# SSD gating and norm inside the first inverse, exponents on ScalarE, and the SSD rows of the output product as f16 products

## What is computed

```python
y = _ssd_chunked(xh, dt, A, Bm, Cm) + d_skip[:, None] * xh      # SSD, 8 heads
y = y.reshape(b, T, SSD_D) * jax.nn.silu(z)                      # gate
y = y.reshape(b, T, SSD_GROUPS, SSD_D // SSD_GROUPS)
y = y * lax.rsqrt(jnp.mean(y * y, axis=-1, keepdims=True) + NORM_EPS)   # group norm
y_ssd = y.reshape(b, T, SSD_D) * norm_g
...
y_rwkv = _rwkv7_mixer(...)                     # a delta rule: needs an inverse per chunk
mix = jnp.concatenate([y_ssd, y_rwkv], axis=-1) @ w_out[l]
h = h + _rms_norm(mix, post_mix_norm[l])
...
u = _causal_dwconv(hn @ ffn_w_up[l], ...)
f = (jax.nn.silu(gate) * val) @ ffn_w_down[l]
```

## Time and profile before

| | us |
|---|---|
| runs, median (lowest, highest) | 769.1 (766.74, 769.5) |
| the profiled execution | 765.5 |
| its span, first to last instruction | 763.7 |
| TensorE busy in the span | 741.5 (97%) |
| VectorE busy | 559.7 (73%) |
| ScalarE busy | 423.1 (55%) |
| GpSimd busy | 61.7 (8%) |

### The profile page before, as it was taken

One profiled execution on the slowest core, in us unless ns is written; L12 is line 12 of the kernel. 1 busy time (PEld: TensorE's weight loads), 2 busy tenths in 40 slices (PEclk: granted clock), 3 DMA queues, 4 the chain that ended last, 5 costly groups with the idle time before them and its releaser, 6 DMA issues.

```text
span 763.7 us, 16837 instructions
## 1 busy us (share of the span) xinstructions
PE 741.5 (97%) x7250; PEld 603.2 (79%) x7250; DVE 559.7 (73%) x906; ACT 423.1 (55%) x673; POOL 61.7 (8%) x104
## 2 busy tenths in 40 slices
PE   9999889889999999999999999999999999999997
PEld 7888777779868888888886777788878888865554
DVE  4799977663978999998666986899766576663443
ACT  6699452222664666667555763297554566653442
POOL 0000123030021011101002000002002000000000
PEclk9999989999999999999999999999999999999999
DMA  9990252111393456545791563338336065555101
GB/s 320 397 369 22 90 213 99 40 61 56 118 323 111 154 180 219 220 169 201 244 389 46 191 247 116 111 112 329 113 111 221 1 221 222 221 220 180 70 1 55
DMA packets 67145, 129.47 MB, mean 170 GB/s; under 512 B 3968, under 2 KB 28032, under 8 KB 66816
## 3 DMA queue, kind: packets, MB, share of 16 engines
q1 hardware_dynamic: 66032, 126.07, 45.4%
q0 software_dynamic: 320, 1.64, 0.6%
q10 hardware_dynamic: 720, 0.70, 0.3%
HBM read 127.35 MB, written 1.05 MB: 168 GB/s over the span
## 4 chain that ended last, share of the span: by engine, by line
PE 65%; DVE 20%; ACT 9%; DMA 3%; issue 2%; SPq 0%; DVEq 0%
PE bank L590 19%; PE bank L706 14%; PE bank L2971 11%; DVE arena L541 8%; DVE arena L2274 3%; PE bank L2361 3%; PE bank L1437 3%; DMA ring<-in_w_in_dram 3%; PE bank L809 2%; PE bank L700 2%; ACT arena L532 2%; PE bank L1456 1%; PE bank L2842 1%; PE bank L2823 1%; PE bank L1694 1%
## 5 line engine op out<-in xcount | busy, mean ns | idle before, releaser
L541 DVE SCALAR_TENSOR_TENSOR arena<-ring,arena 128x1024 f16<-128x1024 f32 x194 | 228.3, 1221 | 71.1 <-ACT arena L532 70.8
L590 PE MATMUL bank<-hg,arena 128*128 128x256 f16 x2496 | 276.1, 273 | 0.9 <-DVE arena L541 0.9
L590 PEld LDWEIGHTS bank<-hg,arena 128*128 128x128 f16 x2496 | 243.0, 98 | 33.3 <-issue 3.1
L532 ACT ACTIVATE arena<-ring 128x1024 f16<-128x1024 f32 x194 | 191.9, 1043 | 88.1 <-PE bank L2971 37.6
L2971 PE MATMUL bank<-arena 128*128 128x512 f16 (+1 forms) x480 | 83.6, 336 | 0.0
L2971 PEld LDWEIGHTS bank<-arena 128*128 128x128 f16 x480 | 47.0, 98 | 36.1
L706 PE MATMUL bank<-arena 128*128 128x256 f16 x528 | 58.2, 273 | 0.2 <-DVE arena L541 0.2
L706 PEld LDWEIGHTS bank<-arena 128*128 128x128 f16 x528 | 51.5, 98 | 6.8 <-issue 0.9
L706 PE MATMUL bank<-mix,arena 128*128 128x256 f16 x480 | 52.9, 273 | 0.0
L706 PEld LDWEIGHTS bank<-mix,arena 128*128 128x128 f16 x480 | 47.0, 98 | 5.7
L590 PE MATMUL bank<-xv,arena 128*128 128x256 f16 x336 | 37.4, 273 | 0.0
(11 more groups left out here) (404 smaller groups left out, 943.1 us busy)
## 6 DMA issues: line engine op xcount, KB each, us to landing
ring<-in_w_in_dram SPq DMA_DIRECT2D x12, 2048.0 KB, 9.9
ring<-in_ffn_w_up_dram SPq DMA_DIRECT2D x22, 1024.0 KB, 7.5
ring<-in_w_ff_dram SPq DMA_DIRECT2D x8, 2048.0 KB, 8.9
ring<-in_w_ff_dram SPq DMA_DIRECT2D x16, 1024.0 KB, 6.1
ring<-in_ffn_w_down_dram SPq DMA_DIRECT2D x11, 1024.0 KB, 6.1
ring<-in_w_out_dram SPq DMA_DIRECT2D x8, 1024.0 KB, 7.4
ring<-in_w_xk_dram SPq DMA_DIRECT2D x2, 2048.0 KB, 11.6
ring<-in_w_xv_dram SPq DMA_DIRECT2D x2, 2048.0 KB, 8.2
```

Source lines behind the costliest of these rows:

```text
L532: nc.scalar.activation(quarter(halves_of(chunk)[0], chunk, q), quarter(slot(*chunk), chunk, q), ACT.Copy, scale=W_SCALE).then_inc(*mark("w ...
L541: nc.vector.scalar_tensor_tensor(quarter(halves_of(chunk)[1], chunk, q), quarter(slot(*chunk), chunk, q), W_SCALE, quarter(halves_of(chunk ...
L590: mm = nc.tensor.matmul(out_, weight[a][:, k, cols], src[:, k, b, :], start=(first and i == 0), stop=(last and i == 2), skip_group_check=True)
```

## The change

The exponents of the SSD go to ACT as `Relu(cumulative - sum)`, followed by `Exp` with scale -1. The four RWKV products on DVE are spread through the SSD stage. Gating moves from ahead of the first inverse to behind its level-0 steps, the squares, sums, rates and end follow in levels 1 and 2. The base products of chunk 1 move to the end of chunk 0. One of the two `y out` copies goes from ACT to DVE. All of `w_out` is now split: quarters 0 and 1 of the SSD rows into the buffer `hg`, the others in place, over quarters of the ring slots that were read. Both slots are given back at the end of the product. In the FFN, `hid high` of a pair comes one step later in ACT's order.

```diff
-        def out1_high(act, qs):
+        def wout_quarter(i, q):
+            if i == 0 and q < 2:
+                return split_view(hg[:, 4 * q:4 * q + 4, :].rearrange("p k t -> p (k t)"))
+            rows, at_ = (0, q + 2) if i and q < 2 else (i, q - 2)
+            return split_view(slot("w_out", "rows", rows)[:, at_, :])
+
+        def wout_high(act, i, qs):
             for q in qs:
-                act.wait_ge(*at("chunk", CHUNK_NO[("w_out", "rows", 1)]))
-                act.wait_ge(*at("y bank", 1, 1))
+                act.wait_ge(*at("chunk", CHUNK_NO[("w_out", "rows", i)]))
+                if i == 0 and q < 2:
+                    act.wait_ge(*at("proj1", 12))
+                else:
+                    act.wait_ge(*at("wout low", *((0, q + 2) if q < 2 else (i, q - 2))))
...
-                if q == 3:
-                    chunk_used("w_out", "rows", 1, ("out1 low", q))
...
+                if name == "w_out" and tail:
+                    chunk_used(name, "rows", 0, used)
+                    chunk_used(name, "rows", 1, used)
...
+            dve_rwkv_bt(dve)
...
-            def exponents(c, g):
-                    nc.vector.tensor_scalar(EX[g][:, i, :], quarters(b)[:, i, :], cstok[:, c, hd:hd + 1], 0.0,
-                                            ALU.subtract, ALU.min).then_inc(
...
+        def act_ssd_exponents(act, c, g):
+            for i in range(4):
+                nc.scalar.activation(EX[g][:, i, :], quarters((1, 2, 3, 7)[2 * c + g])[:, i, :], ACT.Relu,
+                                     bias=cstok[:, c, hd:hd + 1], scale=-1.0).then_inc(
+            nc.scalar.activation(EX[g], EX[g], ACT.Exp, scale=-1.0).then_inc(*mark("ssd_act", "ssd decays", c, g))
...
             products(c, 0, BT, AT_, "LT bank")
-            base_products(c)
             if c == 0:
-                pe_ssd_norm(pe)
-                pe_mem_rates(pe)
-            else:
-                fill(0)
+                base_products(c)
+            fill(0)
...
                 if c == 0 and n == 0:
+                    pe_mem_rates(pe)
+                if c == 0 and n == 2:
                     pe_ssd_rates(pe)
-                    fill(0)
...
                 fill(2 + 2 * n)
+                if c == 0 and n == 1:
+                    pe_ssd_norm(pe)
...
+            if c == 0:
+                base_products(1)
             fill(15)
...
+                if c and n == 0:
+                    mem_low(dve, 5)
+                if c == 0 and n == 0:
+                    dve_ssd_gate(dve, 0)
...
+            if c:
+                wout_low(dve, 1, (0, 1))
+                dve_ssd_low(dve)
...
+            dve.wait_ge(*at("y bank", c, 1))
+            nc.vector.tensor_copy(Y[64:128, :, c * C:(c + 1) * C], quarters(3)[64:128]).then_inc(
+                *mark("solve_vector", "y out", c, 1))
             dve_mem_keys(dve, 2 * c + 1)
...
-            pe.wait_ge(*at("mix1", 3))
+            pe.wait_ge(*at(*(("ssd gated", 0) if i else ("mem", "rstd"))))
...
             narrow(pe, "w_out", KT, mix, lambda k: ("mix1", k), "out1",
-                   lambda b: (("U", 1, 1), ("RB", 1, 1), ("keys", 2), ("keys", 3))[b],
+                   lambda b: (("U", 1, 1), ("RB", 1, 1), ("keys", 3), ("keys", 2))[b],
...
             act_ssd(act)
+            mem_high(act, 1)
             act_mem_rates(act)
-            mem_high(act, 1)
+            act_ssd_squares(act)
             for c in range(NC_):
                 act_rwkv_chunk(act, c)
...
+                if b % 2:
+                    continue
+                if p:
+                    act_hidden(act, p - 1)
```

More of the change, by code:

```diff
@@ L688, in narrow @@
             stored = (name, "rows", 0) in SPLIT_NO
-            split_rows = (0, 1) if name == "w_out_2" else (1,) if name == "w_out" else ()
+            split_rows = (0, 1) if name in ("w_out_2", "w_out") else ()
             for b in range(4):
@@ L720, in narrow @@
                     elif i in split_rows:
-                        pe.wait_ge(*(at("out1 low", kk) if name == "w_out" else at("out low", i, kk)))
+                        pe.wait_ge(*at("wout low" if name == "w_out" else "out low", i, kk))
                     if kk < by_rows:
@@ new lines, in act_ssd_high, with dve_ssd_low @@
+        def act_ssd_high(act):
+            act.wait_ge(*at("ssd out", 3))
+            for i in range(2):
+                nc.scalar.activation(mix16[:, 2 * i:2 * i + 2, 0, :], YN[:, 2 * i:2 * i + 2, :], ACT.Copy).then_inc(
+                    *mark("ssd_act", "ssd high", i))
+        def dve_ssd_low(dve):
+            for i in range(2):
+                dve.wait_ge(*at("ssd high", i))
+                nc.vector.tensor_tensor(mix16[:, 2 * i:2 * i + 2, 1, :], YN[:, 2 * i:2 * i + 2, :],
+                                        mix16[:, 2 * i:2 * i + 2, 0, :], ALU.subtract).then_inc(
+                    *mark("ssd_vector", "mix1", 2 * i))
+                same(("mix1", 2 * i + 1), ("mix1", 2 * i))
@@ L1988, in act_rwkv_chunk @@
                 mem_high(act, 2)
-                for i in range(2):
-                    act_bonus_out(act, i)
+                act_bonus_out(act, 0)
+                act_ssd_root(act)
+                act_bonus_out(act, 1)
                 mem_high(act, 3)
@@ L2297, in split_turn, with act_hidden @@
             return start + (b + 1) // 2 + 1, ((0, 1) if b % 2 else (2, 3)) if b else ()
+        def act_hidden(act, p):
+            for i in range(2):
+                act.wait_ge(*at("hidden float", 2 * p + i))
+                nc.scalar.activation(hid[:, 2 * p + i, 0, :], hidf[p % 2][:, i, :], ACT.Copy).then_inc(
+                    *mark("hidden_high", "hid high", 2 * p + i))
         def act_ffn(act):
```

191 lines of the change are left out of this document (96 added, 95 removed).

## The result

The changed kernel is slower: 776.94 us median of 4 runs (774.28 to 781.49) against 767.92 (766.3 to 769.5, 4 runs) of the kernel before on the same chip, ratio 1.0123, 95% interval 1.009 to 1.0156. The profiled execution took 776.78 us, span 774.9; the one of before 765.5 and 763.7. (My forecast stood on a median of 769.1 for the kernel before, 1.2 us above the 767.92 measured beside the changed one.) All 11.2 us of difference have come up by the end of the FFN's down product (411.38 against 400.14); behind it the two traces run alike. With E for the end of the output product (212.66 before, 217.38 now), 4.7 us have come up by E and 6.5 us behind it.

A forecast was written before the change was run, and what follows sets the result against it. TensorE, busy 97% of the span, was taken as the bound. Terms summed to -3.7 us at full clock, 2.3 us of low clock made it -1.4: 767.7 us against a median of 769.1, range 761.0 to 773.0.

The forecast's parts named there:

- SSD stage: Up to the first inverse: the wait at 84.7 and its low clock go, first inverse starts at 100.2; -2.4 us.
- Hidden, with 1 us to spare: SSD stage: ACT's longer chain ends the last decays at about 96, while TensorE is in the last z tile until 97.
- the 101.5 that I had named as wrong: Sign against the forecast: a first inverse starting after 101.5 would mean ACT's exponents are on the path, not the z tile.
- First inverse: Squares' waits and low clock go, -4.8 us; new waits, 3.5 of them for ACT's bonus, add 5.1; net +0.3 us.
- the -3.4 us for low clock: Start of the first inverse: 3.4 us of low clock go along with 1.4 us of waits for the squares.
- Hand-over and second inverse: Base products cover the y copies, -1.4 us; slightly longer level waits; 1.7 us of low clock counted as gone; -2.6 us.
- Before the product: End of the second chunk: the output product waits for `keys` 3, last in DVE's order; +2.2 us of new waiting.
- product, -3.0: Output product: all products as f16, 96 matmuls in 10.5 us, -3.5; later `y back`, +0.5; together -3.0 us.
- The ring: FFN pair 1 loads only after the output product, delaying ACT's root and the FFN start; +3.9 us, bounds 0 and 6.9.
- FFN, -2.1: FFN pairs: later `hid high` removes ACT's 2.52 and DVE's 0.91 us waits; seven TensorE waits of 0.3 go; -2.1 us.
- Rival C: FFN part does nothing because DVE is held by something else in each pair; 2.1 us stay, 769.8; chance 0.12.
- Rival B: Slower: FFN pair 1 lands after 10.5 us and each of four waits brings low clock; +6.1, 775.2; chance 0.13.

The follow-up runs named there:

- the run with the load held back: Changed kernel with the 4 MB load of w_out held back on SyncE until the first inverse's third level: 778.51 us, ratio 1.0155 to the kernel before.
- the shifted one: Changed kernel with 20 more matmuls of 16 columns in TensorE's warm-up at 1 us, nothing else: 774.77 us, one run.
- the ring run: Changed kernel with ACT's four high halves of FFN pair 1 moved behind the FFN's input: 770.21 us, ratio 1.0022 to the kernel before.

## Why the prediction was wrong, step by step

Forecast 767.7, range 761.0 to 773.0, most likely no change; measured 776.94, slower. The largest single miss is low clock. The sum took the 3.4 and 1.7 us of the old inverses as gone and set 2.3 against them; the profile has 6.9 us in the first inverse (98 to 130) and 5.1 in the second (150 to 180). The next are the FFN's -2.1, of which nothing came, DVE's lead there, the late z tile and the supply of instructions.

- **SSD stage, -2.4, got -0.8.** The wait and the low clock at 84.7 went, as said. The step that failed is "what is late next is the scaling of the last z tile": named, but without a price for the 1.98 us that DVE waits for ACT ahead of it, or for the 1.9 us by which GpSimd's products of L1338 slow DVE on the way. GpSimd's product of r and k took its 2.1 us in both orders. That product alone was held back in a run, and the first inverse then started 2.2 us earlier; how much of the 1.6 us that I missed is ACT's and how much is GpSimd's at 90.8 was not measured apart. The first inverse started at 101.80, past the 101.5 that I had named as wrong, and the reason that I gave for that case holds in part. TensorE does wait for the z tile, but in the profile's chain of work that leads to that matmul ACT's exponents stand ahead of it, from 85.4 to 90.3. "Hidden, with 1 us to spare" was true of TensorE and not of DVE. The table load lies on that chain: 1.28 us, and its next instruction 0.01 us behind, without the drain that the Trainium skill (ScalarE: Activation LUTs, What ACT_TABLE_LOAD costs) counts:

```profile
86.55 1.28 ACT L1303 ACT_TABLE_LOAD   x1
87.84 0.63 ACT L1303 ACTIVATE arena<-arena 128x512 f32<-128x512 f32 x1
```

- **First inverse, +0.3, got +4.1.** The step that failed is the -3.4 us for low clock in the -4.8. The waits came out smaller than forecast: 3.79 us (1.45 + 1.83 + 0.51) against 2.25 before (1.41 + 0.41 + 0.43), so +1.5 for my +3.7. The other +2.6 us are the same matmuls at a lower clock. Low clock came without the squares' waits too, behind the 3.1 us for z: 0.66 between 98 and 108 us. With the gating back in its place and the late z tile ahead, the squares cost 0.36 us. The new wait for the bonus products was real: 1.83 us, and 3.29 where no issue wait stood ahead of it, against 3.5. The term that I did not have is TensorE's supply of instructions, 1.45 us here. In the first inverse of the kernel before no issue wait stands; the sums, few matmuls in much time, lay in that stretch, and the run that put them back lost the issue wait again.
- **Hand-over and second inverse, -2.6, got -0.1; behind it +2.0.** The wait for the copies of y fell from 1.52 to 0.34 as forecast. The gain went to low clock, which I had counted as gone there: 3.4 us between 160 and 180, where the kernel before has none. Issue waits grew from 1.56 us (0.16 and 1.40) to 2.79 (0.56, 1.02 and 1.21). The other profiles in which TensorE has the same program in this stretch tell the two apart. In the five with full clock from 150 to 180 us, the way from the fourth level of the first inverse to the end of the second chunk is 2.0 to 2.7 us shorter than in the kernel before, issue waits and all, as forecast. At 0.67 to 0.91 between 160 and 180 us it is 0.1 to 2.1 us longer, the changed kernel's +1.9 included. So the order of work did what I said, and what failed is the clock, whose scatter from run to run stays unexplained. (The terms written out for this step add up to -2.4, not -2.6.)
- **Before the product, +2.2, got +2.4; product, -3.0, got -2.9.** Both right, also in their mechanism (`y back` 0.28 for 0.5). No low clock followed in this profile. In two others it did: in the run with the load held back and in the shifted one the first 12 matmuls behind the same wait took 2.72 and 2.56 us in place of 1.47.
- **The ring, +3.9, got +4.3.** Right in mechanism: ACT waited 7.17 us, the root came at E + 9.9 for my E + 9.4. That the size fits so well is partly luck of this profile: in six others the root came at E + 11.0 to 11.2, and the second norm total 27.8 to 29.0 us behind E against 26.2 here and 22.0 before, so the term would be +5.8 to +7.0. It was also under-sized in what it does behind: DVE's lead, 0.6 forecast, was some 2 us.
- **FFN, -2.1, got +2.3.** The sign of the step failed. That ACT's and DVE's waits would go was right; that DVE's 9.9 us a pair would stay 9.9 was not. Rival C said this, at 0.12: "DVE is held by something else". GpSimd's low halves had lain in DVE's idle time, and the edit moved them beside its work. Of the 4.4 us between forecast and result 2.1 are this, the rest is the lost lead.
- **Rival B**, the slower side, at 0.13, got the size (775.2) and half of the reason: the pair landed 8 us after E (some 9 in six other profiles), not 10.5, and full clock held in this profile before the product and the FFN. But low clock did come back in both inverses, far beyond the 2.3 us that the forecast had for all of it.

## What to carry to other kernels

An idle time of an engine may hide another engine's work on the same port. Before removing it, look at what runs on GpSimd in that moment: moving the wait moves the collision. When an input comes late, first ask who stands behind the engine that waits for it; a reordering of three lines on ACT gave back 6 to 8 us without touching the load. And where TensorE runs many small matmuls, count them: if one wait is removed and another called "issue" appears 128 matmuls apart, the instruction stream is the bound, and work of few, longer matmuls between the short ones gives it time to catch up.

## What the runs showed of the hardware

- TensorE fetches its instructions in packets of 16 KB, 128 matmuls with their weight loads, on a DMA queue of its own. In the inverses it waited 0.2 to 2.9 us at the ends of these blocks. The Trainium skill (Runtime: NRT & Kernel Launch, Instruction fetch mechanics) gives the same blocks of 256 instructions and calls the cost of crossing into the next "mostly hidden". The first agrees with the trace. The second does not hold here, where 128 matmuls are issued in less time than the 3.5 to 6.0 us between two packets.
- Of two runs with the same wait of 3.1 us before the first inverse, one ran its first 16 matmuls in 2.08 us (the changed kernel) and one in 1.16 (the ring run). Low clock came and went between runs of the same code, and the six profiles with the same code up to there end the fourth level between 129.3 and 132.8 us. A single profile does not price it.
- Beside a GpSimd product of 2.43 us, DVE lost 2.1 us, beside two products of 3.32 us in all 1.9, and beside its two subtractions of 1.5 us in all 0.88.
